# Rows of an expert over 128: tiles of 32 rows in four column quarters instead of tiles of 64 rows in two halves

## The reference

```python
combine = jnp.sum(jax.nn.one_hot(expert_ids, N_EXPERTS, dtype=jnp.float32) * weights[..., None], axis=1)
for e in range(N_EXPERTS):
    h = jax.nn.silu(t @ w_gate[e]) * (t @ w_up[e])
    y = y + combine[:, e:e + 1] * (h @ w_down[e]).astype(jnp.float32)
```

## Time and profile before

| what | value |
|---|---|
| time, median of 3 runs | 923.83 us (923.13 to 925.13) |
| the profiled execution, its own time | 923.86 us |
| its span, first to last instruction | 922.1 us |
| TensorE busy | 866.4 us (94%) |
| VectorE / ScalarE / GpSimd busy | 616.2 / 563.5 / 249.7 us |
| mean granted TensorE clock | 0.973 of full |

### The profile page before, as it was taken

How to read it: one execution, slowest core, us unless ns; L and a number is a source line. 1 busy time by engine, 2 the same in 40 slices (tenths; PEclk the granted TensorE clock), 3 DMA queues, 4 the chain that set the end, 5 groups by cost and what they waited for, 6 DMA issues and landing times.

```text
span 922.1 us, 18021 instructions
## 1 busy us (share of the span) xinstructions
PE 866.4 (94%) x5330; PEld 696.3 (76%) x5331; DVE 616.2 (67%) x1258; ACT 563.5 (61%) x1004; POOL 249.7 (27%) x395
## 2 busy tenths in 40 slices
PE   5899999999999998999973999999999999999994
PEld 4788888898989887788852776776777787677873
DVE  3766666666667667543578866773769599775992
ACT  3664655646373757221241866793889799787991
POOL 5102011010102010000032244543344544455442
PEclk9999999999999998999985899999999999999998
DMA  9800010101010152354473887786598999879973
GB/s 329 257 24 24 25 46 0 45 0 45 0 45 23 47 183 69 138 172 136 149 284 111 321 283 231 249 294 174 218 352 314 324 392 391 272 282 337 393 260 69
DMA packets 54526, 168.41 MB, mean 183 GB/s; under 512 B 9440, under 2 KB 11808, under 8 KB 54496
## 3 DMA queue, kind: packets, MB, share of 16 engines
q1 hardware_dynamic: 47264, 143.13, 41.8%
q0 software_dynamic: 7232, 24.92, 10.4%
HBM read 143.49 MB, written 24.54 MB: 182 GB/s over the span
## 4 chain that ended last, share of the span: by engine, by line
PE 89%; DVE 5%; issue 2%; DMA 2%; ACT 1%; POOL 0%; POOLq 0%; SPq 0%; ACTq 0%; DVEq 0%
PE bank_j L1059 15%; PE bank_j L1061 14%; PE bank_j L1060 14%; PE bank_j L1471 7%; PE bank_j L1121 6%; PE bank_t L1053 4%; PE bank_j L1127 4%; PE bank_s L1487 3%; PE bank_o L1199 3%; PE bank_t L1192 2%; PE bank_s L1059 2%; PE bank_s L1061 2%; PE bank_s L1060 1%; PE bank_o L1061 1%; PE bank_o L1060 1%
## 5 line engine op out<-in xcount | busy, mean ns | idle before, releaser
L1059 PE MATMUL bank_j<-w_high,rows_high 128*128 128x512 f32 x512 | 208.3, 407 | 4.9 <-DVE w_low L1680 2.6
L1061 PE MATMUL bank_j<-w_high,rows_low 128*128 128x512 f32 x512 | 202.6, 396 | 0.0
L1060 PE MATMUL bank_j<-w_low,rows_high 128*128 128x512 f32 x512 | 202.6, 396 | 0.0
L600 POOL TENSOR_TENSOR tick<-mhalf 1x1 f32<-1x1 f32 x176 | 87.8, 504 | 201.8 <-DVE lg L2124 71.8
L1059 PEld LDWEIGHTS bank_j<-w_high,rows_high 128*128 128x128 f32 x512 | 97.7, 191 | 36.3 <-issue 12.1
L2012 DVE TENSOR_TENSOR w_low<-w_res,w_high 128x1024 fp32r<-128x1024 f32 x96 | 114.2, 1219 | 7.0 <-ACT w_high L701 7.0
L1061 PEld LDWEIGHTS bank_j<-w_high,rows_low 128*128 128x128 f32 x512 | 97.8, 191 | 21.3
L1060 PEld LDWEIGHTS bank_j<-w_low,rows_high 128*128 128x128 f32 x512 | 97.7, 191 | 18.7 <-issue 0.2
L701 ACT ACTIVATE w_high<-w_res 128x1024 fp32r<-128x1024 f32 x96 | 97.5, 1050 | 0.8 <-PE bank_j L1061 0.8
L1121 PE MATMUL bank_j<-hnT,w_res 128*128 128x128 f32 x512 | 60.3, 276 | 0.0
L1121 PEld LDWEIGHTS bank_j<-hnT,w_res 128*128 128x128 f32 x512 | 58.4, 192 | 0.9
(11 more groups left out here) (380 smaller groups left out, 1833.5 us busy)
## 6 DMA issues: line engine op xcount, KB each, us to landing
w_res<-in_w_gate_dram SPq DMA_DIRECT2D x48, 512.0 KB, 7.8
w_res<-in_w_up_dram SPq DMA_DIRECT2D x48, 512.0 KB, 7.9
bias<-in_w_down_dram SPq DMA_DIRECT2D x32, 512.0 KB
slot_b<-in_w_gate_dram SPq DMA_DIRECT2D x16, 512.0 KB
PT<-in_w_up_dram SPq DMA_DIRECT2D x16, 512.0 KB
gmix<-in_w_down_dram SPq DMA_DIRECT2D x16, 512.0 KB
h<-in_w_down_dram SPq DMA_DIRECT2D x16, 512.0 KB
hn<-in_x_dram SPq DMA_DIRECT2D x8, 512.0 KB, 3.3
```

What stands on the lines that cost most here:

```text
L600: pool.tensor_tensor(tick[:, len(ticks):len(ticks) + 1], mhalf[0:1, 0:1], mhalf[0:1, 0:1], ALU.mult)
L1059: pe.matmul(out_, ah, bh, start=start, stop=False)
L1060: pe.matmul(out_, ah, bl, start=False, stop=False)
L1061: return pe.matmul(out_, al, bh, start=False, stop=stop)
```

## The change

Half tiles of 64 rows become small tiles of 32 rows. The number of tiles of an expert over its full one becomes ceil((count - 128) / 32). In a small tile 32 of the array's columns are used by a matmul, and four matmuls with results on four quarters of the partitions stand side by side. Gate and up of all 512 hidden columns fit one bank (J0), so there is one silu, one product and one transpose of it. The down matmuls write 256 columns each. Since the weights of 32 rows are now needed on all four quarters of the partitions, PE copies them there with a matmul by a 0/1 matrix (`replicate`, made once by ACT in `GT`), which stands in the middle of gate and up, after k = 4 of 0 to 7; DVE copies its result to `wt_t[:, 1:2]`. `pick_weights` counts on `dve_mh` now, and that matmul waits for it. The tables that hold the rows by tile are laid out for 32 rows.

The core of the diff; first names and sizes:

```diff
-    HP = P // 2
-    HT = S // HP
-    MAXT = NE + (2 * S - 2 * P) // HP
+    QP = P // 4
+    QT = S // QP
+    MAXT = NE + (2 * S - 2 * P) // QP
     TCOLS = NE * S // P + 2
...
+        NL = NE * QT
+        replicate = GT[0:QP, :]
         order_t = sb("tile_order", [P, 1])
```

TensorE:

```diff
-            def half_hidden_T(t, part):
-                pe.wait_ge(dve_mh, 2 * t + part + 1)
-                if part == 0:
-                    wait(pe, dve_hT, 2 * t)
-                pe.transpose((S0, X0)[part][:, 0:P], mh[:, part * P:(part + 1) * P], ident[:, :]).then_inc(pe_hT, 1)
-
-            def half_tile(t, e):
+            def small_tile(t, e):
                 pe.wait_ge(act_raw, t + 1)
                 wait(pe, dve_mh, 2 * t)
 
-                for part, bank in enumerate((J0, J1)):
-                    for k in range(KC):
-                        j, kk = k // 2, k % 2
-                        if part == 0 and kk == 0:
-                            for i in (k, k + 1):
-                                pe.wait_ge(ld_piece[i], e * 16 + (48 if i < OUTP else 32))
-                        cols = [slice(side * HF + part * P, side * HF + (part + 1) * P) for side in range(2)]
-                        for g in range(1 if j < 3 else 2):
-                            for side in range(2):
-                                out_ = bank[side * HP:(side + 1) * HP, 0:2 * P] if j < 3 else \
-                                    bank[side * HP:(side + 1) * HP, g * P:(g + 1) * P]
-                                b = raw_both[j][:, :, kk, cols[side]] if j < 3 else raw_gu[j][g][:, kk, cols[side]]
-                                ins = pe.matmul(out_, raw_rows[:, k, :], b, start=(k == 0), stop=(k == KC - 1),
-                                                skip_group_check=True)
-                        if part == 1 and kk == 1:
-                            ins.then_inc(pe_gup, 1)
-                    if part == 0:
-                        ins.then_inc(pe_gup, 1)
-                half_hidden_T(t, 0)
+                for k in range(KC):
+                    j, kk = k // 2, k % 2
+                    if kk == 0:
+                        for i in (k, k + 1):
+                            pe.wait_ge(ld_piece[i], e * 16 + (48 if i < OUTP else 32))
+                    for g in range(1 if j < 3 else 2):
+                        for q in range(4):
+                            at, cols = slice(q * QP, (q + 1) * QP), slice(q * P, (q + 1) * P)
+                            out_ = J0[at, 0:2 * P] if j < 3 else J0[at, g * P:(g + 1) * P]
+                            b = raw_both[j][:, :, kk, cols] if j < 3 else raw_gu[j][g][:, kk, cols]
+                            ins = pe.matmul(out_, raw_rows[:, k, 0:QP], b, start=(k == 0), stop=(k == KC - 1),
+                                            skip_group_check=True)
+                    if kk == 1:
+                        ins.then_inc(pe_gup, 2 if k == 1 else 1)
+                    if k == KC // 2:
+                        pe.wait_ge(dve_mh, 2 * t + 1)
+                        wait(pe, dve_hT, 2 * t)
+                        pe.matmul(X0[:, 0:1], replicate, wt_t[0:QP, 0:1], start=True, stop=True).then_inc(pe_hT, 1)
                 rows_T(t + 1)
+                pe.wait_ge(dve_mh, 2 * t + 2)
+                pe.transpose(S0[:, 0:P], mh[:, 0:P], ident[:, :]).then_inc(pe_hT, 1)
                 wait(pe, y_ready, 2 * t)
-                for n, c in enumerate(half_order):
-                    if n == 1:
-                        half_hidden_T(t, 1)
-                    if n % 2 == 0:
-                        pe.wait_ge(act_hT, 2 * t + n // 2 + 1)
+                pe.wait_ge(act_hT, 2 * t + 2)
+                for c in range(FC):
                     pe.wait_ge(ld_piece[2 * FC + c], e * 16 + 32)
-                    for side in range(2):
-                        ins = pe.matmul(S1[side * HP:(side + 1) * HP, :], raw_hidden[:, c % 2, c // 2 * HP:(c // 2 + 1) * HP],
-                                        slot[2 * FC + c][:, side * HALF:(side + 1) * HALF], start=(n == 0), stop=(n == FC - 1))
+                    for q in range(4):
+                        ins = pe.matmul(S1[q * QP:(q + 1) * QP, 0:2 * P], raw_hidden[:, c * QP:(c + 1) * QP],
+                                        slot[2 * FC + c][:, q * 2 * P:(q + 1) * 2 * P], start=(c == 0), stop=(c == FC - 1),
+                                        skip_group_check=True)
                     ins.then_inc(pe_dnp, 1)
```

ACT and DVE:

```diff
+            def small_tile(t, h):
 
                 act.activation(warm[:, 0:1], warm[:, 1:2], ACT.Silu)
-                for part in range(2):
-                    act.wait_ge(pe_gup, (FC + 1) * (t + 1) + (1 if part == 0 else FC + 1))
-                    wait(act, dve_mh, 2 * t)
-                    act.activation(sg[:, part * P:(part + 1) * P], (J0, J1)[part][:, 0:P], ACT.Silu).then_inc(act_silu, 1)
-                for part in range(2):
-                    act.wait_ge(pe_hT, 2 * t + part + 1)
-                    wait(act, pe_dnp, FC * (t + 1))
-                    cp(raw_hidden[:, part, :], (S0, X0)[part][:, 0:P]).then_inc(act_hT, 1)
+                act.wait_ge(pe_gup, (FC + 1) * (t + 2))
+                wait(act, dve_mh, 2 * t)
+                act.activation(sg[:, 0:P], J0[:, 0:P], ACT.Silu).then_inc(act_silu, 2)
+                act.wait_ge(pe_hT, 2 * t + 2)
+                wait(act, pe_dnp, FC * (t + 1))
+                cp(raw_hidden[:, :], S0[:, 0:P]).then_inc(act_hT, 2)
                 rows_hi(t + 1)
                 rows_raw(t + 1)
-                weigh_half(t, h)
-
-            def half_tiles(e):
+                weigh_small(t, h)
...
                 dve.tensor_scalar(yb[:, HALF:], O0[:, :], wt_t[:, 0:1], None, ALU.mult).then_inc(y_ready, 1)
 
-            def pick_weights(t):
-                col = dve.value_load(tabi[0:1, bass.ds(t + ROWS, 1)], min_val=0, max_val=2 * TCOLS - 2)
+            def pick_weights(t, picked):
+                col = dve.value_load(tabi[0:1, bass.ds(t + ROWS, 1)], min_val=0, max_val=NL - 1)
                 dve.tensor_copy(wt_t[:, 0:1], lists[:, bass.ds(col, 1), 1:2].rearrange("p a c -> p (a c)"))\
-                    .then_inc(dve_wt, 1)
-
-            def half_tile(t, h):
+                    .then_inc(picked, 1)
+
+            def small_tile(t, h):
                 wait(dve, y_ready, 2 * t)
-                pick_weights(t)
-                for part in range(2):
-                    dve.wait_ge(act_silu, 2 * t + part + 1)
-                    wait(dve, pe_hT, 2 * t)
-                    at = slice(part * P, (part + 1) * P)
-                    dve.tensor_tensor(mh[:, at], sg[:, at], (J0, J1)[part][:, P:2 * P], ALU.mult).then_inc(dve_mh, 1)
+                pick_weights(t, dve_mh)
+                dve.wait_ge(pe_hT, 2 * t + 1)
+                dve.tensor_copy(wt_t[:, 1:2], X0[:, 0:1]).then_inc(dve_wt, 1)
+                dve.wait_ge(act_silu, 2 * t + 2)
+                dve.tensor_tensor(mh[:, 0:P], sg[:, 0:P], J0[:, P:2 * P], ALU.mult).then_inc(dve_mh, 1)
                 dve.wait_ge(act_hT, 2 * t + 2)
                 dve.sem_inc(dve_hT, 2)
                 rows_lo(t + 1)
                 dve.wait_ge(pe_dnp, FC * (t + 2))
                 dve.wait_ge(dve_wt, t + 1)
-                dve.wait_ge(st_half, 16 * h)
-                dve.tensor_scalar(y_half[:, 0:HALF], S1[0:HP, :], wt_t[0:HP, 0:1], None, ALU.mult).then_inc(y_ready, 1)
+                dve.wait_ge(st_small, 16 * h)
+                for q in range(2):
+                    at = slice(q * QP, (q + 1) * QP)
+                    ins = dve.tensor_scalar(y_small[:, q * 2 * P:(q + 1) * 2 * P], S1[at, 0:2 * P], wt_t[at, 1:2], None,
+                                            ALU.mult)
+                ins.then_inc(y_ready, 1)
 
             def tile(t, e, split):
                 for i in range(2 * FC, PIECES):
                     split_lo(e, i)
                 wait(dve, y_ready, 2 * t)
-                pick_weights(t)
+                pick_weights(t, dve_wt)
                 hidden(t, 0)
```

The tables, made ahead of the experts:

```diff
-            NH = HT - 2
+            NH = QT - 4
             thr, more = new(NH), new(NE * NH).rearrange("p (e k) -> p e k", e=NE)
             te, cum = new(NE), new(NE)
-            chain(dve.tensor_scalar(thr, iota_f[:, 0:NH], float(HP), float(P), ALU.mult, ALU.add))
+            chain(dve.tensor_scalar(thr, iota_f[:, 0:NH], float(QP), float(P), ALU.mult, ALU.add))
...
             def list_columns():
 
-                chain(dve.tensor_copy(lists[:, 0::2, :], rows[:, :, :]))
-                top = rows[0:HP, 0:NE * (HT // 2), :].rearrange("p (e c) w -> p e c w", e=NE)
-                low = rows[HP:, 0:NE * (HT // 2), :].rearrange("p (e c) w -> p e c w", e=NE)
-                dve.tensor_copy(upper[:, :, 1:, 0, :], top[:, :, 1:, :]).then_inc(dve_lists, 1)
-                dve.tensor_copy(upper[:, :, :, 1, :], low).then_inc(dve_lists, 1)
-                dve.tensor_copy(lower[:, :, :, 1, :], low).then_inc(dve_lists, 1)
```

(36 more changed lines are left out.)

61 lines of the change are left out of this document (32 added, 29 removed).

## The result

The changed kernel takes 947.93 us (median of 4 runs, 946.93 to 950.82) against 924.19 us of the kernel before beside it: ratio 1.0269, 95% interval 1.0252 to 1.0285. Predicted were 949 us and a range of 936 to 961. The profiled execution took 947.46 us with a span of 945.7 us.

The account below looks back on a forecast made before the run. PE was taken to bound the experts, busy 393.99 of 394.40 us. Small tiles with stalls (+13.7), slow clock (+11.2) and tables (+0.45) gave +25.4 us on 923.86: 949 us, range 936 to 961.

Parts of the forecast that it names:

- The number of tiles and the rate of four column tiles: Experts: 12 small tiles instead of nine half tiles; 0.054 us per instruction of 256 columns, 0.027 for 128.
- A later small tile: Small tile behind another small one: 7.83 us without a stall, 0.55 more if a small one follows.
- The replication's cost: Within gate and up: the replicating matmul's two changes of tiling and two instructions cost 0.45 us per small tile.
- The stall: In eight first small tiles PE waits about 3.2 us for DVE's pick at 5.39 us; such a tile takes 11.32 us.
- The clock: Experts: each of eight stalls is followed by one half-clock stretch of about 3.4 us, costing 1.4 us each, 11.2 in all.
- a rival of its own for all eight: Rival 5: behind the stalls the clock stays at half for a second stretch, another 1.6 us each, 962 us; chance 0.10.
- The sum: Whole kernel: 13.7 us for tiles, 11.2 for the clock and 0.45 ahead of the experts, +25.4 us on 923.86.
- The tables: Ahead of the experts: larger comparison of counts with thresholds and the sum over it cost 0.45 us before the first gather.
- The clock that stays (938): Rival 2: the stall comes in first tiles but the clock stays full, 938 us; chance 0.20.
- No stall (910): Rival 3: the pick is there when PE comes, a first tile takes 7.83 us, 910 us in all; chance 0.06.
- Matmuls that can't be fed faster than 0.055 us (960): Rival 4: small tiles' instructions step no faster than 0.055 us, 0.9 us more per tile, 960 us; chance 0.12.
- 968 by the prediction's estimate: Small tiles' 80 gate and up and 32 down instructions stepping at 62 ns, by the skill's microcode decoding: 968 us.

Follow-up runs that it names:

- the wait alone: Kernel before, with one wait added: in a half tile PE waits after k = 4 for DVE's pick of the weights; 961.83 us, ratio 1.0430.
- the late replication: Changed kernel with the replicating matmul behind the first group of down matmuls and DVE's product ahead of its pick; 917.63 us, ratio 0.9926.
- the column tiles: Changed kernel with the replication at the same place as four matmuls of 32 columns instead of one of 128; 944.01 us, ratio 1.0216.
- nine tiles: Changed kernel with tile-count thresholds 64 rows apart, so nine small tiles run and rows beyond are left out; 924.23 us, ratio 1.0006.
- the two late versions: Changed kernel with replication behind the first down matmuls, 917.63 us; the same with four narrow matmuls and without ACT's 0/1 matrix, 914.88 us.
- The kernel with the stalls of 2.0 us: Changed kernel with the replicating matmul behind k = 7 instead of k = 4; 939.93 us, ratio 1.0177.

## Why the prediction was right

**The number of tiles and the rate of four column tiles.** 12 and 9, as worked out. Forty instructions of 256 columns step at (2.37 - 0.38) / 39 = 0.051 us (0.054 assumed, and 0.053 given as the least: it is a little less), those of 128 columns at 0.22 / 8 = 0.0275 (0.027). A later small tile with a small one behind it:

```profile
642.28 2.37 PE L1465 MATMUL bank_j<-w_res,rows_raw 128*32 128x256 f32 x40 [0.36 <-ACT rows_raw L699]
...
644.58 0.38 PE L1472 MATMUL bank_x<-wt_t,GT 32*128 32x1 f32 x2
...
644.89 0.64 PE L1465 MATMUL bank_j<-w_res,rows_raw 128*32 128x256 f32 x8
...
646.00 0.40 PE L1465 MATMUL bank_j<-PT,rows_raw 128*32 128x128 f32 x8
...
649.87 0.38 ACT L699 ACTIVATE rows_raw<-bank_t 128x256 f32<-128x256 f32 x1 [0.86 <-DVE rows_low L2106]
...
650.59 2.37 PE L1465 MATMUL bank_j<-w_res,rows_raw 128*32 128x256 f32 x40 [0.39 <-ACT rows_raw L699]
```

Gate and up end 4.12 us behind the start (4.18 predicted), the next small tile starts 4.19 us behind that (4.20), a full one 3.73 (3.65). A later tile takes 7.85 us (7.83). Inside the second half two small errors cancel: the down matmuls start at 1.87 us, not 1.58, since ACT's copy starts and is taken up later than assumed (PE waits 0.69 us for it), and from there to the next tile it is 1.86 us, not 2.07.

**The replication's cost.** 0.45 us was assumed; with the replication moved out of the way gate and up end at 3.67 instead of 4.12 us, 0.45. The 0.17 us per change of shape was read from a row of weight loads, where PE itself was not idle, so the row was thin support; the runs give 0.38 us for the two. The Trainium skill's "TensorEngine Tiling (Array Packing)", section "Tiling Modes", says that a change of mode drains the engine; the run with four narrow matmuls in its place agrees, with 0.38 us saved.

**The stall.** Pick at 5.37 to 5.50 us (5.39 predicted), eight times, 26.2 us of idle time, 3.28 each (about 3.2). At full clock a first tile took 11.27 us (11.32). The run with the wait alone and the one with the late replication show it as the cause from both sides.

**The clock.** Eight falls at 1.4 us, 11.2 us, were predicted. Six of eight stalls were followed by one, and the first tiles of 102.5 us together lie 11.3 us above five of 11.27 and three of 11.61. Four of the falls cost 1.1 to 1.6 us, 1.4 in the mean, as priced. The total was right by two errors that cancel, which is luck: fewer falls, but two of them longer than one stretch (15.1 and 13.7 us, at a mean clock of 0.66 and 0.75; 3.5 and 2.4 us lost), which the prediction had as a rival of its own for all eight. One of its reasons was thin: that no fall followed the idle 1.6 us at 474.4 says little, since PE worked only 0.4 us before it was idle again, and a wait of 1.54 us for a gather was followed by a fall in the late replication.

**The sum.** 134.5 - 110.3 = 24.2 us in the small tiles (by their starts to 0.01 us) against 24.9 predicted (13.7 + 11.2). The tables cost what was said, here the comparison, 0.62 us instead of 0.39:

```profile
495.09 0.62 DVE L1529 TENSOR_TENSOR hnT<-off_e,qk_vm 128x448 f32<-128x448 f32 x1
```

The sum over them grew alike: from the thresholds to `row_g`, which the first gather needs, it is 2.38 us instead of 1.90, 0.48 more (0.45 predicted). All the same the experts start 1.7 us earlier in this execution: an early part of the program, which the change doesn't touch, ran at a clock of 0.62 from 44.8 to 49.2 us in the profiled execution before and at 1.00 in this one. The seven experiments' starts lie between 506.0 and 508.9 us too. At the end 0.6 us more pass behind the start of the last full tile, the full tile of the expert with the slowest small one takes 0.4 us more, and the first full tile 0.1. Together 23.6 us between the profiled executions.

**The rivals.** The clock that stays (938): out, though it held behind two stalls. No stall (910): it is what the changed kernel would be with the replication elsewhere, and even then 915 to 918, since a gather becomes late next. Matmuls that can't be fed faster than 0.055 us (960): out, 96 instructions of 256 columns in a row stepped at 0.051 us and 32 of 128 columns at 0.0275. The Trainium skill's "TensorE: Matmul & The Clock Gate", section "Wait — 56ns, not 53.3ns?", gives 62 ns per matmul for decoding in microcode (968 by the prediction's estimate); the same steps speak against it here. What was left open: why the clock fell behind six of eight equal stalls and not behind the other two. The profiled runs with the same stall or nearly the same have six of eight as well (the wait alone, the column tiles) or eight of eight (nine tiles). The runs show that idle time is the cause, not which idle time is enough.

## What to carry to other kernels

When a value is wanted earlier than before, look at when its maker delivers it today, even if nobody waited for it: a row of idle time that costs nothing on one engine becomes the bound once the busiest engine stands behind it. Put a small operation with a late input at the last place where its result is still in time, behind work that is ready, and in the shape that its neighbours have. And finer tiles pay only if the cost per tile falls by more than their number grows: here the number grew by a third, and a tile without a stall fell from 12.2 to 7.85 us, but with the stall it took 11.3 to 15.1.

## What the runs showed of the hardware

In the profiled executions a stall of 2.0 us lowered the clock as often as one of 3.25 us (six of eight); with the same 3.25 us in the kernel of nine small tiles it was eight of eight. Of six waits of 0.8 to 1.6 us for a gather, in the two late versions, two were followed by a fall. A fall cost 1.1 to 3.5 us on top in the changed kernel. The kernel with the stalls of 2.0 us had the widest spread of its own times, 933.6 to 942.3 us; why is not shown. A replicating matmul of another shape cost 0.45 us among column tiles of 128x32, the same by four matmuls of their shape 0.07. Four column tiles of 256 columns ran at 0.051 us per instruction, half of two tiles' 0.106, with no loss over 96 instructions.
